# The first block's mixing: attention heads in groups of four, output norm by query, projections woven with attention

## What is computed

```
def _mixing(h, w_in, qn_a, kn_a, qn_c, kn_c, sinks, g_out, w_o, cos, sin):
    qa, ka, va, qi, ki, wi, qb, kb, vb, qc, kc, vc = split(h @ w_in)
    qa, ka, qc, kc = rope(rms(each)); qi, ki = rope(each)
    oa = _dsa(qa, ka, va, qi, ki, wi)      # score = sum_h wi*relu(qi.ki); top-k; softmax
    ob = _stick_breaking(qb, kb, vb)       # exp(log_sigmoid(z) + sum of log_keep behind)
    oc = _swa_sinks(qc, kc, vc, sinks)     # m = max(s, sink); e = exp(s - m)
                                           # p = e / (sum(e) + exp(sink - m)); p @ v
    o = _rms(concat([oa, ob, oc]), g_out)  # over the 64 values of each head
    return o @ w_o
```

## Time and profile before

| | us |
|---|---|
| median of three runs | 3590.11 (3590.05 to 3600.42) |
| the profiled execution | 3598.64 |
| its span | 3596.7 |
| PE busy in the span | 3285.6 (91%) |
| DVE, ACT, POOL busy | 1871.5, 723.7, 723.6 |
| mixing of layer 0 (from 61.2 to 533.7) | 472.5 |
| mixing of layer 1 (from 976.9 to 1451.4) | 474.5 |

### The profile page before, as it was taken

One profiled execution on the slowest core, in us unless ns is written; L12 is line 12 of the kernel. 1 busy time (PEld: TensorE's weight loads), 2 busy tenths in 40 slices (PEclk: granted clock), 3 DMA queues, 4 the chain that ended last, 5 costly groups with the idle time before them and its releaser, 6 DMA issues.

```text
span 3596.7 us, 33796 instructions
## 1 busy us (share of the span) xinstructions
PE 3285.6 (91%) x12184; PEld 2199.1 (61%) x12184; DVE 1871.5 (52%) x4154; ACT 723.7 (20%) x1593; POOL 723.6 (20%) x580
## 2 busy tenths in 40 slices
PE   6978989999998798999997997899997999889997
PEld 3434537888743453688883453388884444368886
DVE  1495537775329653577632266286742337153343
ACT  2124421000112432100002242220112133121110
POOL 0000013344200000244440000134441000124442
PEclk8987789999999757999999977899998978989998
DMA  4111313443211000254321100144430210012121
GB/s 191 70 47 71 117 55 109 175 177 109 88 47 71 1 1 35 82 181 170 141 79 53 71 24 0 59 151 156 174 117 32 89 47 1 24 70 94 71 94 47
DMA packets 38548, 304.91 MB, mean 85 GB/s; under 512 B 4192, under 2 KB 4320, under 8 KB 23920
## 3 DMA queue, kind: packets, MB, share of 16 engines
q1 hardware_dynamic: 38352, 302.68, 22.9%
q0 software_dynamic: 32, 0.07, 0.0%
HBM read 300.63 MB, written 2.10 MB: 84 GB/s over the span
## 4 chain that ended last, share of the span: by engine, by line
PE 81%; DVE 12%; issue 3%; ACT 2%; DMA 1%; POOL 0%; SPq 0%; DVEq 0%; POOLq 0%; ACTq 0%
PE bank L847 42%; PE bank L825 21%; PE bank L987 2%; PE bank L1003 2%; PE bank L993 1%; PE bank L1144 1%; DVE SPT L2031 1%; PE bank L968 1%; DVE sel L1726 1%; PE bank L922 1%; PE bank L1128 1%; DVE m L1725 1%; DMA ring<-in_slabs 1%; PE bank L909 1%; PE bank L1135 1%
## 5 line engine op out<-in xcount | busy, mean ns | idle before, releaser
L825 PE MATMUL bank<-hT,ring 128*128 128x512 f32 x1600 | 715.2, 606 | 32.4 <-issue 21.3
L788 POOL TENSOR_TENSOR SPT<-ring 128x512 f32<-128x512 f32 (+2 forms) x140 | 168.6, 1204 | 2790.2 <-DMA ring<-in_slabs 2168.6
L825 PEld LDWEIGHTS bank<-hT,ring 128*128 128x128 f32 x1600 | 308.1, 193 | 435.0 <-issue 429.7
L847 PE MATMUL bank<-U,ring 128*128 128x256 f32 x1728 | 406.5, 380 | 0.0
L847 PEld LDWEIGHTS bank<-U,ring 128*128 128x128 f32 x1728 | 326.3, 190 | 43.3
L1551 DVE SCALAR_TENSOR_TENSOR nw<-sel,c,nw 128x256 f32<-128x256 f32 x504 | 325.7, 646 | 25.7 <-DMA sel<-in_mod_pieces 8.0
L847 PE MATMUL bank<-hT,ring 128*128 128x256 f32 x1216 | 298.1, 396 | 23.4 <-ACT hT L1405 8.7
L847 PE MATMUL bank<-U,SPT 128*128 128x256 f32 x1296 | 311.3, 379 | 1.4 <-POOL SPT L793 1.4
L847 PE MATMUL bank<-hT,SPT 128*128 128x256 f32 x1216 | 287.3, 379 | 0.0
L847 PEld LDWEIGHTS bank<-hT,ring 128*128 128x128 f32 x1216 | 229.7, 195 | 71.1 <-issue 17.2
L847 PEld LDWEIGHTS bank<-U,SPT 128*128 128x128 f32 x1296 | 246.1, 190 | 35.6 <-POOL SPT L793 2.2
(11 more groups left out here) (275 smaller groups left out, 4004.9 us busy)
## 6 DMA issues: line engine op xcount, KB each, us to landing
ring<-in_slabs SPq DMA_DIRECT2D x88, 2048.0 KB, 8.0
sel<-in_mod_pieces SPq DMA_DIRECT2D x144, 512.0 KB, 3.9
ring<-in_slabs SPq DMA_DIRECT2D x8, 1536.0 KB, 7.3
ring<-in_slabs SPq DMA_DIRECT2D x8, 1280.0 KB, 6.1
ring<-in_slabs SPq DMA_DIRECT2D x4, 1664.0 KB, 6.9
ring<-in_slabs SPq DMA_DIRECT2D x2, 1808.0 KB, 7.4
cst<-in_consts SPq DMA_DIRECT2D x1, 2120.0 KB, 23.9
ring<-in_slabs SPq DMA_DIRECT2D x2, 1056.0 KB, 5.2
```

What stands on the lines that cost most here:

```text
L788: pool.tensor_tensor(e1, a21, a22, ALU.add).then_inc(*pool_order.up())
L825: mm = pe.matmul(dst, lhs(k), rhs(k), start=(k == 0), stop=(k == n - 1))
L847: mm = pe.matmul(into[j][:, c:c + HALF], lhs[:, k, :], rhs[:, k, :], start=(begin and k == 0), stop=(end and k == kp - 1))
```

## The change

- Tiles are made in another order, `TILES1`: the "c" tiles before the "a" queries and "b" tiles, with the weight slabs regrouped to fit.
- The 48 units become 14 groups: eight of four "c" heads (one query tile each) and six "a" groups of four or two heads. Scores of even heads go to bank 2 and of odd heads to bank 3, from the two halves of the rows of the array. The weights are not divided by their sum. The value product takes the transposed weights as stationary operand (128 columns) and the values as moving one (64 columns), so its output is 128 queries by 64 columns a head, on bank 6.
- The output norm is taken there: ACT squares, DVE reduces over the 64 columns of each head and folds the sum of the weights in (EPS times its square), ACT takes Ln and Exp, DVE refines (`root_step`) and multiplies; `ot` (PE, 24 a layer, and 8 `bot` of stick attention) transposes the result back, and ACT copies it with the gain as scale. The stage of the output norm (L1009) goes.
- Stick attention works on a whole head at once (one flat strip of 1280 columns instead of four pieces), and POOL does its small mask operations.
- POOL also makes two of the four products of `pss` and the cosine product of `rope`, and DVE waits for them. For the indexer ACT applies Relu and DVE accumulates.
- Banks are dealt by kind: 0 and 1 for projections, 2 and 3 for scores, 4 and 5 for transposes, 6 for outputs, and 7 for pss, rope, ot, bot, and the later mg and mp.
- The list: eight tiles, projv, idx and 12 top-k rounds; then the other eight tiles, the "c" groups and 36 rounds woven; then stick attention, the "a" groups, in layer 0 the modulation products, and the first half of `wo` (its four "c" feature tiles) woven; then the second half of `wo`. A tile's product is cut in four parts, `pj`, between which other steps may stand.
- The load of the second block's positions and the feed-forward part's first slab sums wait for later points of the list.

The core of the diff:

```diff
+PROJ, ROWS, TURN, OUT, SMALL = (0, 1), (2, 3), (4, 5), (6,), (7,)
...
+TILES1 = (0, 1, 2, 3, 10, 11, 12, 13, 14, 15, 4, 5, 6, 7, 8, 9)
+ROPED = [n for n in TILES1 if n not in (6, 7, 8, 9)]
+NORMED = [n for n in ROPED if n > 2]
+SLAB_OF_TILE = {n: (("qi", "kq", "qa", "qb")[k // 4], k % 4) for k, n in enumerate(TILES1)}
...
+GROUPS1 = [("c", 4 * kv, 4, i) for kv in range(2) for i in range(QT)]
+GROUPS1 += [("a", 0, 4, 0), ("a", 0, 4, 1), ("a", 0, 2, 2), ("a", 2, 2, 2), ("a", 0, 2, 3), ("a", 2, 2, 3)]
+NC1 = 2 * QT
...
+def woven(*streams):
+
+    out = []
+    for start, end, chunks in streams:
+        for n, chunk_ in enumerate(chunks):
+            out.append((start + (end - start) * (n + 0.5) / len(chunks), chunk_))
+    return [st for _, chunk_ in sorted(out, key=lambda x: x[0]) for st in chunk_]
...
+def group_slots(groups):
+
+    out = []
+    for j in range(len(groups) + 3):
+        slot = []
+        if j < len(groups):
+            slot.append(("sc", groups[j]))
+        if 0 <= j - 1 < len(groups):
+            slot.append(("tp", groups[j - 1]))
+        if 0 <= j - 3 < len(groups):
+            slot.append(("on", groups[j - 3]))
+        if 0 <= j - 2 < len(groups):
+            slot.append(("pv", groups[j - 2]))
+        if 0 <= j - 3 < len(groups):
+            slot.append(("ot", groups[j - 3]))
+        out.append(slot)
+    return [[st] for slot in out for st in slot]
...
+    def tile(m):
+        n = TILES1[m]
+        return [("pj", n, 0), ("pj", n, 1), ("pj", n, 2), ("proj", n)]
...
+    for m in range(8):
+        o += tile(m) + side(m)
...
+        if m == 5:
+            o += [("idx", i, hp) for i in range(1, QT) for hp in range(2)]
+        if m >= 6:
+            o += [st for chunk_ in rounds[:6] for st in chunk_]
+            rounds = rounds[6:]
+    dense = []
+    for m in range(8, 16):
+        steps = tile(m)
+        dense += [[st] for st in steps[:-1]] + [[steps[-1]] + side(m)]
+    dense += [side(16), side(17)]
+    o += woven((0.0, 0.92, dense), (0.24, 1.0, group_slots(range(NC1))),
+               (0.0, 1.0, rounds + [[("seldone", i)] for i in range(1, QT)]))
+    mods = []
     if l == 0:
-        o.append(("modb",))
-    for t in range(8 + 1):
-        if t < 8:
-            o.append(("osq", t))
-        if t >= 1:
-            o.append(("on", t - 1))
-    o += [("wo", n) for n in range(KT)]
+        for s in range(MOD_FIRST, MOD_SLABS):
+            mods += [[("mg", s)], [("mp", s)]]
+        mods.append([("modb",)])
+    o += woven((0.0, 0.95, stick_slots()), (0.0, 0.95, group_slots(range(NC1, len(GROUPS1)))),
+               (0.0, 0.55, mods), (0.55 if l == 0 else 0.1, 1.0, [[("wo", 0, n)] for n in range(KT)]))
+    o += [("wo", 1, n) for n in range(KT)]
...
+    if kind == "pj":
+        return [(("proj", st[1]), PROJ)] if st[2] == 0 else []
+    if kind == "projv":
+        return [(st, PROJ)]
+    if kind == "wo":
+        return [(st, PROJ if st[1] else PROJ[:1])]
+    if kind == "bpv":
+        return [(st, PROJ[1:])]
+    if kind == "pv":
+        return [(st, OUT)]
+    if kind in ("sc", "idx"):
+        return [((kind,) + st[1:] + ("even",), ROWS[:1]), ((kind,) + st[1:] + ("odd",), ROWS[1:])]
+    if kind == "bz":
+        return [(st + (0,), ROWS[:1]), (st + (1,), ROWS[1:])] if st[2] == 0 else [(st + (0,), ROWS[:1])]
+    if kind == "br":
+        return [(st + (0,), TURN[:1]), (st + (1,), TURN[1:])] if st[2] == 0 else [(st + (0,), TURN[:1])]
+    if kind == "tp":
+        return [(st + (j,), TURN[j:j + 1]) for j in range(len(chunks_of(GROUPS1[st[1]])))]
+    if kind in ("pss", "rope", "ot", "bot"):
+        return [(st, SMALL)]
+    if kind in ("mg", "mp"):
+        return [(st, SIDE if st[1] < MOD_FIRST else SMALL)]
...
+                    if kind == "pss":
+                        k = normed_at[st[1]]
+                        pool.wait_ge(*s1["prs"].after(l, k + 1))
+                        pool_link(pool.tensor_tensor(tmp[:, 1, :], rb[:, k % 2, :], rb[:, k % 2, :], ALU.mult))
+                        pool.tensor_tensor(nw[:, k % 2, :], nw[:, k % 2, :], tmp[:, 1, :], ALU.mult).then_inc(
+                            *s1["pa"].up())
+                        pool.wait_ge(*s1["pa"].now())
+                    elif kind == "rope":
+                        n = st[1]
+                        pool.wait_ge(*bk1.ready(l, st))
+                        pool.tensor_tensor(PT[:, n, :], PT[:, n, :], cst[:, C_COS:C_COS + SEQ], ALU.mult).then_inc(
+                            *s1["pc"].up())
...
+                        pe.wait_ge(*s1["ex"].after(l, g + 1))
+                        for part, (a, z) in enumerate(chunks_of(GROUPS1[g])):
+                            b = bk1.bank(l, st + (part,))
+                            for m in range(a, z):
+                                j, hh = m // nh, m % nh
+                                mm = pe.transpose(bank[b][:, P * (m - a):P * (m - a) + P],
+                                                  rowS[g % 2][:, P * (nk * hh + j):P * (nk * hh + j) + P], ident)
+                            mm.then_inc(full[b], 1)
+                    elif kind == "pv":
+                        g = st[1]
...
+                        for hh in range(nh):
+                            for j, kb in enumerate(ks):
+                                m = j * nh + hh
+                                mm = pe.matmul(dst[:, HD * hh:HD * hh + HD], rowT[g % 2][:, P * m:P * m + P],
+                                               VT[:, kb, v:v + HD], start=(j == 0), stop=(j == len(ks) - 1))
                         mm.then_inc(*done)
...
+                    elif kind == "ot":
+                        g = st[1]
+                        pe.wait_ge(*s1["un"].after(l, g + 1))
+                        for t in range(GROUPS1[g][2] // 2):
+                            mm = pe.transpose(dst[:, P * t:P * t + P], onat[g % 2][:, P * t:P * t + P], ident)
                         mm.then_inc(*done)
...
+                        if g >= 2:
+                            act.wait_ge(*s1["uv"].after(l, g - 1))
+                        act.activation(osq[g % 2][:, 0:n], src[:, 0:n], ACT.Square).then_inc(*s1["uq"].up())
+                    elif kind == "on":
+                        g = st[1]
...
+                        act.wait_ge(*s1["uv"].after(l, g + 1))
+                        act.activation(stat[:, 24:24 + nh], stat[:, 20:20 + nh], ACT.Ln).then_inc(*act_order.up())
+                        act.wait_ge(*act_order.last())
+                        act.activation(stat[:, 24:24 + nh], stat[:, 24:24 + nh], ACT.Exp, scale=-0.5).then_inc(*s1["ur"].up())
...
-            def normed(l, t, g, k):
-
-                a = tmp[:, 1, :]
-                if s1["pn"].seen:
-                    dve.wait_ge(*s1["pn"].now())
-                link(dve.tensor_tensor(a, rb[:, k % 2, :], rb[:, k % 2, :], ALU.mult))
-                link(dve.tensor_tensor(a, a, nw[:, k % 2, :], ALU.mult))
-                link(dve.scalar_tensor_tensor(t, t, g, rb[:, k % 2, :], ALU.mult, ALU.mult))
-                return dve.scalar_tensor_tensor(t, a, 1.5, t, ALU.add, ALU.mult)
+            def root_step(v, r, t):
+
+                link(dve.tensor_tensor(t, r, r, ALU.mult))
+                link(dve.scalar_tensor_tensor(t, t, -0.5, v, ALU.mult, ALU.mult))
+                link(dve.scalar_tensor_tensor(r, t, 1.5, r, ALU.add, ALU.mult))
...
+                        t = PT[:, n, :]
+                        link(dve.scalar_tensor_tensor(t, t, vec[:, g:g + 1], rb[:, k % 2, :], ALU.mult, ALU.mult))
+                        dve.wait_ge(*s1["pa"].after(l, k + 1))
+                        dve.scalar_tensor_tensor(t, nw[:, k % 2, :], 1.5, t, ALU.add, ALU.mult).then_inc(*s1["pn"].up())
...
+                            link(dve.tensor_tensor(total, total, stat[:, 12:16], ALU.add))
+                        link(dve.scalar_tensor_tensor(stat[:, 16:16 + nh], total, EPS, total, ALU.mult, ALU.mult))
+                        dve.wait_ge(*s1["uq"].after(l, g + 1))
+                        link(dve.tensor_reduce(v, osq[g % 2][:, 0:HD * nh].rearrange("p (h d) -> p h d", h=nh), AX.X, ALU.add))
+                        dve.scalar_tensor_tensor(v, v, 1.0 / HD, stat[:, 16:16 + nh], ALU.mult, ALU.add).then_inc(
+                            *s1["uv"].up())
                     elif kind == "on":
...
+                        dve.wait_ge(*s1["ur"].after(l, g + 1))
+                        if g >= 2:
+                            dve.wait_ge(*bk1.ready(l, ("ot", g - 2)))
+                        root_step(stat[:, 20:20 + nh], stat[:, 24:24 + nh], stat[:, 28:28 + nh])
+                        b = bk1.bank(l, ("pv", g))
+                        dve.tensor_tensor(onat[g % 2][:, 0:HD * nh].rearrange("p (h d) -> p h d", h=nh),
+                                          bank[b][:, 0:HD * nh].rearrange("p (h d) -> p h d", h=nh),
+                                          stat[:, 24:24 + nh].unsqueeze(2).broadcast_to([P, nh, HD]),
```

(1 more changed line is left out.)

638 lines of the change are left out of this document (368 added, 270 removed).

## The result

The changed kernel takes 3539.61 us (median of four runs, 3535.37 to 3541.65) against 3594.55 us of the kernel before, measured beside it. The ratio is 0.9836 with a 95% interval of 0.9819 to 0.9854: faster by 1.6%, 55 us between the medians. The forecast was 3480 us, a gain of 112, so the direction held, the time lies inside the range, and half of the gain is missing. The profiled execution took 3541.45 us (span 3539.7), 57 us under the 3598.64 of before.

What follows compares the result with a forecast made beforehand. TensorE, busy 91% of 3596.7 us, was taken as the bound, so gains come from its idle time or vanishing work. Layer 1 -59.5 and layer 0 -52.5 give -112: 3478 against the median, said as 3480, range 3380 to 3600.

Steps and rivals of the forecast that it cites:

- the forecast's band: Whole kernel: the forecast's own case, 3430 to 3540 us, most likely 3480, chance 0.48.
- engines in step: Rival, woven stages: PE works about 65%, waits cost 25 us more each, 50 per layer; 3540 to 3580 us, chance 0.17.
- Front part: Eight tiles, value projection, indexer and 12 top-k rounds of each layer: 89.4 + 20.4 + 2.5 = 112 us.
- bank-7 term: Front part: rope product waits for ScalarE's read of the sum of squares on shared bank 7; 0 to 5.6, taken 2.5 us.
- The tile: Front part: each of two added projection tiles with norm and rope costs 7.7 to 10.95 us, taken as 10.2.
- Prices of the pieces: PE's cost per four-unit group at full clock: scores 1.3 to 2.5 us, transposes 1.5, value products 2.0, turning back 0.4.
- The woven stages: Dense stage 140 us (bounds 110 and 165); last stage 118 in layer 1 (bounds 96 and 143), 130 in layer 0.
- the choice I called weakest: Woven stages: how much of them PE works, chosen from rows of other stages; 76% in the dense stage.
- clock term: Addition for TensorE not running at full clock: 16 us in layer 1 and 9 in layer 0.
- the 3487 of the sum: Whole kernel: the profiled 3598.6 us less the gain of 112, before moving down to the median (3478).
- The slower rival: Woven stages run at half clock: layer 1 541 us, layer 0 some 565, 3750 in all; chance 0.13.
- the break-even: Slower rival: the gain of 112 is eaten with 34% to 63% of the stages' PE work at half clock.

Runs made afterwards that it cites:

- late start: Kernel with two output banks and the late turn, its first window groups starting at 0.30 of the dense stage instead of 0.24: 3501.56 us, ratio 0.9726.
- late turn: Kernel with two output banks, a group's output turned back (ot) four slots behind its scores instead of three: 3505.48 us, ratio 0.9759.
- the seam: Changed kernel with one woven stage in place of two, aimed at the stretch where the two stages meet: 3546.42 us, ratio 0.9864.
- the idle products: Changed kernel with 46 extra TensorE products per layer, results overwritten, ahead of other steps: 3590.27 us at 512 columns, 3551.44 us at 128.

## Why the prediction came out so

The direction and the kind of mechanism held: the output norm's stage and the softmax stretch at 0.55 went, and the weaving carried the gain. The gain was 55 us where 112 were forecast. 3539.61 lies at the very edge between the forecast's band (to 3540) and that of the engines in step (from 3540), so the number alone doesn't tell these apart.

**Front part.** 112 against 113.2 and 114.9. The total came out, but by two errors that cancel. The bank-7 term was too small: the rope product waited 1.47 us behind ScalarE each time, as priced from the earlier trace rows, and the run with its own bank gave back 5.9 us where I took 2.5 of at most 5.6. The tile was too dear: from one rope product to the next are 10.3 us with that wait in them, so 8.9 without it, where I took 10.2.

```profile
1063.05 1.12 PE L1059 MATMUL bank<-U,cst 128*128 128x512 f32 x2 [1.47 <-ACT rb L1435]
1064.02 7.03 PE L1039 MATMUL bank<-hT,ring 128*128 128x512 f32 x16
1070.88 1.02 PE L1051 MATMUL bank<-sqb,cst 128*128 128x512 f32 x2
1073.38 1.13 PE L1059 MATMUL bank<-U,cst 128*128 128x512 f32 x2 [1.47 <-ACT rb L1435]
```

**Prices of the pieces.** These came out at or under the bounds. In the timeline at full clock:

```profile
1106.52 1.13 PE L1120 MATMUL bank<-U 64*128 64x256 f32 x8
...
1182.70 1.04 PE L1133 MATMUL bank<-cst,SPT 128*128 128x128 f32 x8
```

(A score or value product leaves two records, a transpose one.) Four heads' scores take 1.13 us, less than half of four in a row, so the halves of the array do work at once (1.3 was the low end); eight transposes 1.04 instead of 1.5; eight value products 2.00 (the first row of the timeline further up), as the L916 row said. The Trainium skill ("TensorEngine Tiling (Array Packing)", When to Use Tiling) would keep the 64-wide operand stationary; this trace has 0.25 us each against 0.29 before, so nothing was lost against the kernel before by the reverse. What packing such operands two at a time would give, no run here tests.

**The woven stages.** 140 and 118 were forecast in layer 1, 153.5 and 139.9 came. The share that PE is busy, the choice I called weakest, reads as taken, 76% and 82% for 76% and 79%, but that is partly luck: the forecast's share was of work at full clock, and the measured one holds what half clock adds. Busy time times granted clock is about 95 + 87 = 182 us of work at full clock, where I had 107 + 93 = 200, so by the forecast's own measure the two stages work 62% of their time. Half clock costs the rest of the busy time, 21 + 27 = 48 us. The idle time is 37 + 26 = 63, where I had 33 + 25 = 58. So the **clock term, 16 us, is the mis-sized one**: it was 48. In layer 0 it was 9 and is 21 + 26 = 47. Together the clock was 70 us too small. The work came out 34 us lower (182 for 200, and 207 for 223 with layer 0's modulation products), the idle time 13 higher, the rest (front parts, second halves, the feed-forward stretch) some 5 higher: 54 us, which is what the profiled execution lies above the 3487 of the sum. (The product of busy time and clock is a rough measure, but it gives 183 us for the kernel without weaving and 178 for the one with the late start, which have the same products of PE.) Three of the 18 us of work in layer 1 are a slip of the sum: stick attention's 43.2 us busy at 0.79 are 34 us of work, not 37. The error in the clock was to take the clock of stretches that consist of large products for stages in which PE waits every few us; the earlier trace rows had the warning, 0.79 in stick attention and 0.55 in the softmax stretch, and the 0.99 of 360 to 400 was read for a rule.

**The slower rival.** Its price was right in kind. 48 us lost on 182 us of work is a quarter of the work done at half clock; the break-even was put at 34% at the least. So the case came three quarters of the way and no further. The clock itself read between the two signs: over 0.85 was the forecast's, 0.55 to 0.6 this rival's, and 0.76 to 0.82 came. Without the weaving (clock 0.76 and 0.68) the change is slower than before, but that is not this rival's case: the idle time grew there by 42 us in layer 1 and the half-clock loss by 24.

**Engines in step.** This rival had the place right and the price wrong: the one output bank is held from value product to norm, but the idle time of layer 1 was 5 us above the forecast, not 50. Giving the groups a second bank, together with the rope product apart from the sum of squares (9 us when done alone), took 29 us off the mixing, about half of what was missing. Idle time fell little with it (7 us), busy time at a higher clock did (22). What remains is spread over hand-overs: the other edits (late turn, later start, POOL's share, the seam) moved the wait to the next one or did nothing that is clear of noise.

**Transposes and the clock.** The Trainium skill ("TensorE: Matmul & The Clock Gate", Part 4) says that transposes do not count as PE work the way matmuls do. The same number of transposes stands in kernels with 0.68 and with 0.83 in the last stage of layer 1, so the order of the steps and the waits in it move the clock at a fixed number of them; what the transposes add, no run here separates. Whether half clock is a cause of its own also stays open: the idle products raised it and lost the gain to their own work, they could not fill the waits for the banks, and in the other runs clock and waits changed together.

## What to carry to other kernels

Cost a woven stage as three terms, work at full clock, waits, and work again times the share at half clock, and bound the third from both sides: the stretch of before with the largest products (0.87 here) and those with the most hand-overs (0.79 and 0.55). The woven stages came between them, at 0.76 to 0.82; the best of the rows alone was too kind, and 0.55 would have been far too hard. In a pipeline whose engines walk one list, count for each accumulator bank the steps between its writing and its release, and what unrelated steps stand between them on each engine: a 0.2 us step behind other streams' copies came 5.6 us late while the one output bank was held. The new deal of banks took 29 us off; moving POOL's products to VectorE changed nothing in the changed kernel. When one wait is removed, name the next before counting the gain.

## What was not expected of the hardware

Four score products of 64 rows in pairs on the two halves of the array took 1.13 us where four units' had taken 4 x 0.63 = 2.5; the forecast had allowed for 1.3 at best. Idle products of 128 columns, a quarter of the size, raised the granted clock of layer 1's dense stage from 0.82 to 0.87, nearly as far as large ones did (0.88 to 0.89).
